# A two-block network on one core: zeros stored behind other loads, loads asked for in turns, one head mixed ahead of a dot, three more idle products

## The reference

```python
mod = silu(c) @ w_ada + b_ada                 # 6 x 1024 values that shift, scale and gate
sh1, sc1, g1, sh2, sc2, g2 = split(mod, 6)
h = rmsnorm(x) * (1 + sc1) + sh1
q, k, v, u = split(h @ w_in)
attn = rmsnorm((softmax(q1 k1) - lam * softmax(q2 k2)) @ v)     # 4 heads, causal
y = S5(u); z = gelu(y); ssm = z * sigmoid(z @ w_glu + b_glu)
x = x + g1 * (concat(attn, ssm) @ w_out)      # "x mixed", 8 row tiles
h = rmsnorm(x) * (1 + sc2) + sh2
logits = h @ w_router + b_router; top 4 of 32, softmax      # routing
x = x + g2 * moe(h)                           # each expert: (clip(up) + 1) * swish(gate) @ w2
... second block: mod_2 = silu(c_2) @ w_mod_2 + b_mod_2, and so on
```

## Time and profile before

| what | value |
|---|---|
| median of three runs | 2104.07 us |
| the profiled execution | 2103.96 us, of which its span is 2102.6 |
| PE busy | 2012.3 us, 96% |
| DVE, ACT busy | 629.9 us (30%), 404.6 us (19%) |
| DMA | 553.79 MB, mean 263 GB/s |
| mean granted clock of PE | 0.98 |
| chain that ended last | PE 65%, DMA 14%, waits in SP's queue 12%, DVE 5% |

### The profile page before, as it was taken

The page is one execution under the profiler, slowest core; times in us unless marked ns, Lnnn a source line. Parts: engine busy times, 40 slices in busy tenths (PEclk is TensorE's granted clock), DMA queues, the critical chain, the costliest instruction groups (busy, mean ns, idle before and its releaser), DMA issues.

```text
span 2102.6 us, 36384 instructions
## 1 busy us (share of the span) xinstructions
PE 2012.3 (96%) x15877; PEld 909.7 (43%) x15877; DVE 629.9 (30%) x1252; ACT 404.6 (19%) x837; POOL 51.9 (2%) x54
## 2 busy tenths in 40 slices
PE   8999898989999999999999999989999999999998
PEld 4555444333433344443333334355444444444443
DVE  5979765111111111111111111133453444300002
ACT  3224412111111010111110101012333343300001
POOL 0000000000000000000000000030000000000000
PEclk9999997999999999999999999979999999999999
DMA  8753687999799999999999999871212211122202
GB/s 322 269 203 130 258 296 284 407 412 375 318 414 408 420 403 415 402 410 408 406 407 412 408 414 416 371 261 62 103 64 67 70 63 64 62 70 80 79 31 70
DMA packets 107666, 553.79 MB, mean 263 GB/s; under 512 B 13361, under 2 KB 24625, under 8 KB 57713
## 3 DMA queue, kind: packets, MB, share of 16 engines
q1 hardware_dynamic: 87392, 517.36, 62.0%
q10 hardware_dynamic: 14560, 17.28, 2.5%
q0 software_dynamic: 5552, 16.78, 2.3%
HBM read 526.73 MB, written 26.35 MB: 263 GB/s over the span
## 4 chain that ended last, share of the span: by engine, by line
PE 65%; DMA 14%; SPq 12%; DVE 5%; issue 2%; ACT 1%; DVEq 0%
PE psum L875 17%; PE psum L1055 13%; SPq L414 12%; PE psum L1062 10%; DMA arena<-in_w 8%; PE psum L883 7%; PE psum L552 4%; DMA ring<-in_w 3%; PE psum L1011 3%; PE psum L1125 3%; DMA ring<-in_dot_slabs 2%; DMA arena<-in_mod_slabs 1%; DMA ring<-in_mod_slabs 1%; PE psum L869 1%; PE psum L1103 1%
## 5 line engine op out<-in xcount | busy, mean ns | idle before, releaser
L875 PE MATMUL psum<-arena,ring 128*32 128x512 f32 x4096 | 453.8, 595 | 17.2 <-DMA arena<-in_w 16.6
L875 PEld LDWEIGHTS psum<-arena,ring 128*32 128x32 f32 x4096 | 137.3, 110 | 329.5 <-issue 326.2
L1055 PE MATMUL psum<-h_t,ring 128*128 128x512 f32 x640 | 278.6, 592 | 0.3 <-ACT arena L1429 0.3
L883 PE MATMUL psum<-arena,h_t 128*32 128x256 f32 x3840 | 216.7, 383 | 10.6 <-DMA arena<-in_w 9.7
L1949 DVE TENSOR_SCALAR h_t<-psum 128x512 f32<-128x512 f32 (+2 forms) x33 | 27.9, 845 | 614.5 <-PE psum L875 614.5
L1356 ACT ACTIVATE ring<-psum,mods,gain 128x64 f32<-128x64 f32 (+2 forms) x264 | 85.6, 428 | 650.4 <-PE psum L861 650.4
L1055 PEld LDWEIGHTS psum<-h_t,ring 128*128 128x128 f32 x640 | 120.4, 190 | 146.4 <-issue 145.9
L883 PEld LDWEIGHTS psum<-arena,h_t 128*32 128x32 f32 x3840 | 122.7, 110 | 95.6 <-DMA arena<-in_w 14.3
L875 PE MATMUL psum<-ring 128*32 128x512 f32 x1344 | 149.4, 593 | 7.6 <-DMA ring<-in_w 7.6
L552 PE MATMUL psum<-h_t,ring 128*128 128x512 f32 x256 | 118.5, 618 | 2.6 <-ACT h_t L1176 2.6
L1062 PE MATMUL psum<-h_t,ring 128*128 128x512 f32 x256 | 112.6, 593 | 1.4 <-ACT work L1240 1.4
(11 more groups left out here) (432 smaller groups left out, 1733.3 us busy)
## 6 DMA issues: line engine op xcount, KB each, us to landing
arena<-in_w SPq DMA_DIRECT2D x288, 1024.0 KB
ring<-in_w SPq DMA_DIRECT2D x96, 1024.0 KB
ring<-in_dot_slabs SPq DMA_DIRECT2D x40, 512.0 KB, 5.4
ring<-in_turn_slabs SPq DMA_DIRECT2D x40, 512.0 KB, 3.3
ring<-in_merge_slabs SPq DMA_DIRECT2D x32, 512.0 KB, 3.3
ring<-in_mod_slabs SPq DMA_DIRECT2D x6, 2048.0 KB, 13.3
ring<-in_proj_slabs SPq DMA_DIRECT2D x24, 512.0 KB, 4.1
y_rows<-arena SPq DMA_DIRECT2D x3, 3584.0 KB, 18.7
```

The costliest lines, as they stand in the source:

```text
L875: mm = pe.matmul(psum[32 * j:32 * j + 32, g, :], x_e[:, c * tokens + g * TG:c * tokens + g * TG + TG], slot[s][:, j * S:(j + 1) * S], star ...
L883: mm = pe.matmul(psum[32 * j:32 * j + 32, 6 + g // 2, (g % 2) * 256:(g % 2) * 256 + 256], h_e[:, g * 256 + half * P + 32 * c:g * 256 + hal ...
L1055: mm = pe.matmul(psum[:, bank, :], ring[:, s, k, :], h_t[:, k, :], start=(k == 0), stop=(k == KT - 1))
```

## The change

On SP the three stores of zeros, which stood one each ahead of the loads of slabs 8, 9 and 10, now stand behind the loads of dots 0 to 3. Later on SP, dots 24 to 31 and slabs 20 to 23 are asked for in another order, and chunks 6 and 10 no longer follow each other. On DVE the mixing of head 1 stands ahead of dot 12, and the sixteen dots 24 to 39 are spread over the eight steps of "x mixed" otherwise. On PE `keep_on(1, 3)` in the routing is now `keep_on(4, 3)`. No instruction is added or removed beside these three products.

```diff
-            sp.wait_ge(sem("zeros set"), 1)
             for n, at in zip(range(8, 11), ((2, 1), (3, 0), (3, 1))):
-                clear_blocks(7 * (n - 8), 7 * (n - 7))
                 load_slab_of(n)
                 load_mod_half(*at)
...
             load_slab_of(11)
             load_dots(0, 1, 2, 3)
+            sp.wait_ge(sem("zeros set"), 1)
+            for n in range(3):
+                clear_blocks(7 * n, 7 * n + 7)
             for n in range(12, 16):
                 load_slab_of(n)
...
             load_dots(20, 21, 22, 23)
-            load_dots(24, 25, 26)
-            for n in range(20, 24):
+            load_dots(24, 25, 26, 27)
+            for n in range(20, 23):
                 load_slab_of(n)
+            load_dots(28, 29, 30, 31)
+            load_slab_of(23)
             sp.wait_ge(sem("head mixed"), 4)
-            load_dots(27, 28, 29, 30)
-            load_first(6, 10)
-            load_dots(31, 32, 33, 34)
+            load_dots(32, 33)
+            load_first(6)
+            load_dots(34, 35)
+            load_first(10)
+            load_dots(36, 37)
             load_first(11)
-            load_dots(35, 36, 37, 38, 39)
+            load_dots(38, 39)
...
             turn_rows(TT - 1)
-            keep_on(1, 3)
+            keep_on(4, 3)
...
-            dots(7, 13)
+            dots(7, 12)
             masked_head(3)
             head_mixed(1)
...
-            dots(13, 16)
+            dots(12, 16)
             normal(3)
...
-                dots(*((24, 24), (24, 24), (24, 28), (28, 32), (32, 35), (35, 38), (38, 40), (40, 40))[k])
+                dots(*((24, 25), (25, 26), (26, 28), (28, 31), (31, 34), (34, 37), (37, 39), (39, 40))[k])
```

## The result

The changed kernel took 2086.9 us, the median of four runs (2084.9 to 2087.15), beside 2103.7 for the kernel before (four runs, 2099.84 to 2105.54): a ratio of 0.9924, 95% interval 0.9907 to 0.994. That is 16.8 us less; 2089.0 was forecast. The profiled execution took 2086.84 us, its span 2085.5, 17.1 less than before.

What follows compares the result with a forecast made beforehand. The experts' stage, nearly full on DMA and PE, was to keep its length and move with its first product; 4.1 + 8.6 + 2.3 = 15.0 us off 2103.96 gave 2089.0, range 2086.8 to 2090.6 (8 in 10: 2085.0 to 2093.3).

Steps and rivals of the forecast that it cites:

- Stores of zeros behind the dots: PE's waits on modulation halves (2, 1) and (3, 1) go, so DVE's first S5 output starts earlier: 4.1 us.
- Head 1 mixed ahead of dot 12: PE's wait for head 1's mixing goes (5.81 us) and its clock stays up (2.8 more): 8.6 us.
- the two certain terms: The gains from moving the zero stores, 4.1 us, and from mixing head 1 ahead of dot 12, 8.6 us.
- (e): Rival: one of the two certain terms fails by an unseen wait; 2093.1 without the first, 2097.6 without the second; chance 0.08.
- Dots and slabs in turns: End of routing: last logits 2.7 us earlier, gather 3.6 earlier, less a clock charge of 1.3: net 2.3 us.
- the lower of my two ends: Gather in the routing: 1.9 us earlier if the chunks' backlog alone decides; the other end was 7.0.
- charge of 1.3 for the clock: PE idles before the tokens come, so its half clock lasts longer there: 1.3 us off the turns' gain.
- Three idle products: In PE's gap ahead of the token rows (L849): cost nothing, gain nothing.
- (b): Rival: ACT's stores get their share at once, fourth row tile lands 7.0 earlier: 2085.6; chance 0.12 together with (c).
- (c): Rival: idle products hold PE's clock into the experts' first pass: 2085.6; chance 0.12 together with (b).
- (a): Rival: the turns bring nothing, by late dots at step 7, the backlog or a colder PE: 2091.3; chance 0.18.
- (d): Rival: the zeros block the queue, PE is 14.6 us late at slab 12: 2107.7, slower; chance 0.04.

Runs made afterwards that it cites:

- a1_stores: The kernel before with only the three stores of zeros moved behind dots 0 to 3: 2100.45 us, ratio 0.9985.
- a2_head: The kernel before with only head 1 mixed ahead of dot 12: 2096.62 us, ratio 0.9966.
- a3_turns: The kernel before with only SP's new order of dots, slabs and chunks and the new spread of dots on DVE: 2100.36 us, ratio 0.9992.
- b2_late_chunks: The changed kernel with chunks 12 to 15 asked for only when all four row tiles are stored: 2085.0 us, ratio 0.9923.
- b5_no_table: The changed kernel with the old table of dots per step on DVE, SP's new order kept: 2082.36 us, ratio 0.9896.
- b6_no_sporder: The changed kernel with SP's old order of loads, the new table of dots kept: 2088.36 us, ratio 0.9926.
- b1_one_idle: The changed kernel with one idle product instead of four in the routing: 2087.52 us, ratio 0.9933.
- a4_idle: The kernel before with only the idle products in the routing raised from one to four: 2097.83 us, ratio 0.998.
- b3_late_one_idle: The changed kernel with chunks 12 to 15 asked for after all row tiles are stored, and one idle product instead of four: 2085.49 us, ratio 0.9922.
- b4_late_bridge: b3_late_one_idle plus six idle products on PE ahead of the wait for the gathered tokens: 2089.88 us, ratio 0.9937.
- b8_gather_first: The changed kernel with chunks 12 to 15 asked for only when both first gathers have landed: 2087.97 us, ratio 0.9926.

## Why the prediction was right

**Stores of zeros behind the dots.** Forecast 4.1, measured 4.26, and 4.0 with that part alone. The signs named for it came: no wait of PE on either half, the S5 output at 135.76 (135.9 forecast), no wait of ACT for "y cleared", the last zeros landed near 157.7 (155 forecast). Slab 12 took 24.1 us to land and was there at 159.0 (158 forecast), 17 us ahead of PE. One size inside the term was off: a half was to land in 7.3 us without a store ahead of it, and half (2, 1) took 8.7 (9.6 before), 9.2 in a1_stores, where PE still waited 0.26. For half (3, 1), which carries most of the gain, it was 7.6 (12.7 before). The gain is also less certain than one pair of executions makes it look. Without the moved stores the S5 output lay between 139.44 and 143.49 in four profiled executions, with them between 134.14 and 137.42 in ten; the means are 5.7 us apart.

**Head 1 mixed ahead of dot 12.** Forecast 8.6, measured 9.01: PE's L671 at 225.49 is 10.29 earlier than L666 was, of which 4.26 are the stores, so 6.0 for the wait; slab 15 gave 2.54 and L671 itself 0.49. The clock was the part that might have failed, and it stood at 1.00. a2_head shows the same 8.96 by itself up to slab 23, so up to there the two certain terms add without touching each other, and (e) falls.

**Dots and slabs in turns.** The net of 2.3 came out near (1.93 + 0.50 = 2.43 at the first product of the experts), and that was luck: it was made of three numbers, and two were mis-sized, one too high as a gain and one too high as a cost. The last logits came 2.87 earlier behind slab 23 (2.7 forecast). Of this the gather got 1.93, where I took 3.6: the backlog of chunks alone decided, the lower of my two ends. In the ten kernels that don't ask for chunks 12 to 15 late, the gather stood 26.9 to 27.5 us behind the issue of the first three chunks, also in a3_turns, where the first row store stood 5.2 us behind the chunks instead of 9.6. When they are late, as in b2_late_chunks, it went out 5.95 us earlier, so the backlog is shown to be the bound. The charge of 1.3 for the clock wasn't paid. The first 64 products even ran 0.8 us faster (8.37 against 9.16), as the clock was back at full speed some 4 us behind the first tokens on PE (0.50 from 336 to 337, 0.95 in the next microsecond), where 5.9 were read from the trace of before. The 0.50 is not the transfer's: the gather took 3.3 us to land where it took 2.9 before. But before, PE's own half-clock work ended after the tokens were there (348.6 against 347.6), and now it ends ahead of them. 1.9 + 0.5 + 0.8 are 3.2 where 2.3 stood.

b5_no_table and b6_no_sporder say which half did it: SP's order brings the 2.87 and would bring the experts 5.96 us forward alone; the table, which I had walked through as part of the gain, takes 3.5 of them back (3.3 from the start of the span) by holding back the chunks. The line for it was in my working ("Dot 39 now ends at 315.6, so the chunks start 1.9 earlier"); I read it as a gain and never asked what the old table would give under the new order.

**Three idle products.** Forecast nothing; b1_one_idle shows nothing, in either direction, and a4_idle no more than 1.1 us. That they are free hangs on the wait for the stored rows: in b3_late_one_idle, where the row numbers release the gather, leaving them out gave 2.1 us. In the changed kernel all four took 5.62 us, and the row numbers came 20.5 us behind the last logits instead of 18.7 in b1_one_idle, both well ahead of the gather at 27.1.

**The sum.** 4.26 + 9.01 + 1.93 + 0.50 = 15.70 to the first product of the experts, against 15.0 forecast to the end. Their stage kept its length within 0.5 us (1023.96 to 1023.45), as the argument needed. The 0.89 behind it is smaller than what that stretch does by itself from run to run. 2086.9 is 2.1 below the forecast and 1.3 above the 2085.6 of the rivals (b) and (c), so the time can't choose between them; the marks do.

**The rivals.** (a), the turns bring nothing, falls: the last logits came 2.87 us earlier behind slab 23, without a wait. One of its signs did show, 1.57 us of waiting for a dot in step 5, but DVE was still ready 0.42 us ahead of PE's next slab. (b), the stores served as soon as they are issued, would have had the gather at 325; it came at 329.48, so it falls. By the Trainium skill, "DMA: Bandwidth & Descriptors", section "Queues, rings and completion order", a DMA engine turns from queue to queue packet by packet. The trace agrees only loosely: ACT's row stores of 0.5 MB took 11.0 us in the median beside SP's chunks and 6.4 once four of them were gone. (c), the idle products hold the clock, falls: the clock was at 0.52 from 330 to 336, behind the idle products and a wait of 3.04 us. By the Trainium skill, "TensorE: Matmul & The Clock Gate", section "What's actually happening", the slow clock is the default and activity lifts it; b4_late_bridge agrees: its clock rose from 0.50 to 1.00 within the bridge, and the first 64 products took 7.07 us. It also shows that lifting it cost more than it gave. (d), the zeros block the queue, falls: the stores did land one behind the other, but 8.6 and 8.7 us apart, near the 8.8 that their bytes take in a full window, and not 22.5 each.

## What to carry to other kernels

When work is spread over more steps, look for every wait on its total. Here a wait for all 40 dots stood ahead of 7 MB of loads, so moving one dot into the last step held all of them back, and the even table cost 3.3 us. Where the next stage is bound by its transfers, starting it earlier isn't enough: if bytes that it needs are asked for only after the queue has fallen idle, the stage gets longer by what is still to come of them when its own loads begin. And when a change has several parts, run the whole without each of them, not only each part alone: a3_turns showed a gain of both halves together and hid that one of them works against the other.

## What the hardware showed beside that

An issue can hold SP for many microseconds. The issues of the three stores of 3.7 MB (L343) took 11.39 us of SP's queue, where four dots of 0.5 MB took 1.75. The third issue alone took 10.22 us, and 10.2 to 11.1 in all ten kernels that have the three in a row; in the four that have them apart, none took more than 0.94. What it waits for is not shown. It cost nothing here, as slab 12 was there 17 us ahead of PE; a load behind it that is due would be late by it.

Most of what differs from run to run lies behind the experts. From their end to the end of the span the profiled runs took 722.4 us (b4_late_bridge) to 736.2 (a3_turns), while the experts' stage itself, b8_gather_first aside, varied by 2.7. In that stretch PE's idle products stand behind a pause that the profile puts down to nothing that it shows ("issue"): 3.17 us in the changed kernel, 3.16 in b4_late_bridge, 2.93 and then another 8.68 in b3_late_one_idle (735.7 us), whose line is the first here. In b4_late_bridge the clock was still at 1.00 after the pause, and the next products took 1.96 us for four, in the second line; in the changed kernel, in the third, they ran at half clock, 3.75.

```profile
1370.98 2.05 PE L571 MATMUL psum<-consts 128*128 128x512 f32 x2 [8.68 <-issue]
```

```profile
1367.17 1.96 PE L571 MATMUL psum<-consts 128*128 128x512 f32 x4 [3.16 <-issue]
```

```profile
1362.19 3.75 PE L570 MATMUL psum<-consts 128*128 128x512 f32 x4 [3.17 <-issue]
```

No part of this change touches that stretch, and it differed by up to 14 us between two profiled executions. A change of 3 us, as the turns, is told by marks near its place and not by the time of a few runs. Why the pause is longer in some runs stays open.
